# Two routed expert blocks: all six raw weight slots asked for before the passes, and the gathered rows split between the first two weight pieces

## The reference, cut to what matters

```
# moe_swiglu: each token goes to its best 2 of 8 experts
logits = xt @ w_router + b_router; top_logit, top_e = top_k(logits, 2); top_w = softmax(top_logit)
for each block of rows of one expert e:
    xb = xt[toks]
    h = silu(xb @ w_gate[e]) * (xb @ w_up[e])          # 1024 x 1408 twice
    out = (h @ w_down[e]) * w                          # 1408 x 1024
y[token] += out
# hier_moe: each token goes to its best group of 4, and to 2 experts in it
hid = silu(t @ w_gate[e]) * (t @ w_up[e]) * combine[e] # per expert 1024 x 256 twice
y = sum over e of hid @ w_down[e]                      # 256 x 1024
```

## Time and profile before

| | |
|---|---|
| median of the runs | 2325.05 us |
| profiled execution, its own time | 2320.53 us |
| its span, first to last instruction | 2319.0 us |
| PE / PEld busy | 2068.7 us (89%) / 1570.0 us (68%) |
| DVE / ACT / POOL busy | 1285.5 us (55%) / 994.2 us (43%) / 185.8 us (8%) |
| `moe` norm, plan, passes begin | 1059.7, 1085.3, 1105.1 us |
| `hm` norm, plan, passes begin | 2062.8, 2093.4, 2110.0 us |
| DMA rate, last three of the 40 slices of 58 us | 399, 373, 258 GB/s |

### The profile page before, as it was taken

How to read it: one execution, slowest core, us unless ns; L and a number is a source line. 1 busy time by engine, 2 the same in 40 slices (tenths; PEclk the granted TensorE clock), 3 DMA queues, 4 the chain that set the end, 5 groups by cost and what they waited for, 6 DMA issues and landing times. The chain is left out here.

```text
span 2319.0 us, 31287 instructions
## 1 busy us (share of the span) xinstructions
PE 2068.7 (89%) x11611; PEld 1570.0 (68%) x11611; DVE 1285.5 (55%) x1814; ACT 994.2 (43%) x1308; POOL 185.8 (8%) x182
## 2 busy tenths in 40 slices
PE   7966898889999989997899999997898789686998
PEld 5743334668888877876777888786476359575776
DVE  3367746353133234444566666888367745525888
ACT  2135736342223222221566665774243643404774
POOL 0010000000000000000311010111112200002111
PEclk9978988989999999997899999999999789886999
DMA  8006101144144125002778777995320000126996
GB/s 249 6 14 237 47 10 45 37 127 123 43 122 127 37 83 194 1 37 83 256 269 282 278 270 281 370 391 216 88 73 28 12 1 1 74 84 174 399 373 258
DMA packets 220713, 336.29 MB, mean 145 GB/s; under 512 B 50413, under 2 KB 135309, under 8 KB 220606
## 3 DMA queue, kind: packets, MB, share of 16 engines
q1 hardware_dynamic: 213470, 314.53, 40.0%
q0 software_dynamic: 7136, 20.34, 2.3%
HBM read 306.82 MB, written 26.95 MB: 144 GB/s over the span
## 5 line engine op out<-in xcount | busy, mean ns | idle before, releaser
L1526 DVE TENSOR_TENSOR moe_pass_wL<-moe_pass_w,moe_pass_wH 128x2048 fp32r<-128x2048 f32 (+1 forms) x144 | 303.4, 2112 | 115.8 <-ACT moe_pass_wH L1450 111.3
L1450 ACT ACTIVATE moe_pass_wH<-moe_pass_w 128x2048 fp32r<-128x2048 f32 (+1 forms) x144 | 254.7, 1772 | 129.6 <-PE PS L557 97.2
L555 PE MATMUL PS<-moe_pass_wL,moe_pass_xgH 128*128 128x512 f32 (+1 forms) x384 | 148.3, 386 | 9.1 <-DVE moe_pass_xgL L1531 4.8
L1526 DVE TENSOR_TENSOR hm_pass_wL<-hm_pass_w,hm_pass_wH 128x2048 fp32r<-128x2048 f32 x60 | 135.9, 2288 | 34.8 <-ACT hm_pass_wH L1450 34.7
L555 PE MATMUL PS<-xnT_low,ffn_upH 128*128 128x512 f32 x352 | 140.3, 399 | 7.4 <-DVE xnT_low L873 7.1
L557 PE MATMUL PS<-moe_pass_wH,moe_pass_xgH 128*128 128x512 f32 (+1 forms) x384 | 143.5, 374 | 0.0
L556 PE MATMUL PS<-moe_pass_wH,moe_pass_xgL 128*128 128x512 f32 (+1 forms) x384 | 143.5, 374 | 0.0
L557 PE MATMUL PS<-ffn_xH,ffn_upH 128*128 128x512 f32 x352 | 139.9, 397 | 0.0
L556 PE MATMUL PS<-ffn_xH,ffn_up_low 128*128 128x512 f32 x352 | 138.4, 393 | 0.0
L1450 ACT ACTIVATE hm_pass_wH<-hm_pass_w 128x2048 fp32r<-128x2048 f32 x60 | 112.2, 1910 | 17.1 <-PEq L1340 6.0
L880 DVE TENSOR_TENSOR ffn_hT<-ffn_sg,PS 128x512 f32<-128x512 f32 x22 | 15.1, 688 | 167.7 <-PE PS L557 167.7
(11 more groups left out here) (841 smaller groups left out, 4868.6 us busy)
## 6 DMA issues: line engine op xcount, KB each, us to landing
moe_pass_w<-in_moe_w_down SPq DMA_DIRECT2D x40, 1024.0 KB, 4.9
moe_pass_w<-in_moe_w_gate SPq DMA_DIRECT2D x32, 1024.0 KB, 5.2
moe_pass_w<-in_moe_w_up SPq DMA_DIRECT2D x32, 1024.0 KB, 7.2
hm_pass_w<-in_exp_w_gate SPq DMA_DIRECT2D x40, 512.0 KB, 7.7
hm_pass_w<-in_exp_w_up SPq DMA_DIRECT2D x40, 512.0 KB, 6.9
hm_pass_w<-in_exp_w_down SPq DMA_DIRECT2D x40, 512.0 KB
od_W<-in_od_w_in SPq DMA_DIRECT2D x12, 1024.0 KB, 8.2
moe_pass_w<-in_moe_w_gate SPq DMA_DIRECT2D x16, 768.0 KB
```

What stands on the lines that cost most here:

```text
L555: nc.tensor.matmul(out, lh, rl, start=start, stop=False)
L1450: nc.scalar.activation(wH[:, i % S, 0:n], w[:, i % R, 0:n], ACT.Copy).then_inc(s["high"], 1)
L1526: nc.vector.tensor_tensor(wL[:, i % S, 0:n], w[:, i % R, 0:n], f32(wH[:, i % S, 0:n]), ALU.subtract) \
```

## The change: what it does

`first` asks for all `R` = 6 items instead of two, in `moe` in the plan stage and in `hm` in the norm stage, so in `hm` 12 DMAs of 512 KB instead of 4 stand ahead of the four stores of `xs`. The four loads at the passes' start are gone. On ACT the rows' rounding `xg_high` goes between `high(0, 0)` and `high(0, 1)` in `hm` alone; in `moe` (where `OVER` is 32) ACT's order stays. On DVE `xg_low` goes between `low(0, 0)` and `low(0, 1)` in both. The passes after the first and the loop's body are as they were.

```diff
@@ class ExpertWeights @@
     def first(self, sp, e):
-        for i in range(self.AHEAD):
+        for i in range(self.R):
             self.load(sp, e, i)
@@ sorted_passes, block.sync @@
             n = passes(sp)
-            e = expert(sp, 0)
-            for i in range(AHEAD, R):
-                ring.load(sp, e, i)
@@ sorted_passes, block.scalar @@
             high(0, 0)
-            high(0, 1)
+            if OVER:
+                high(0, 1)
             xg_high(0, OVER > 0)
+            if not OVER:
+                high(0, 1)
@@ sorted_passes, block.vector @@
             low(0, 0)
+            xg_low(0)
             low(0, 1)
             if NW:
                 dve.sem_inc(s["cw"], 1)
-            xg_low(0)
```

## The result

The changed kernel took **2309.05 us** (2304.84 to 2317.68, six runs) beside 2322.74 for the kernel before (2315.34 to 2329.28, six runs): ratio 0.9947, 95% interval 0.9922 to 0.9973. Forecast were 2317.8 us and a range of 2312.5 to 2323.5: right in sign, too small, and outside the range. The profiled execution took 2309.62 us (span 2307.9) against 2320.53 (2319.0): 10.9 us less. Over all 13 executions of the changed kernel in this study the mean is 2311.3 us, over 100 of the kernel before 2323.7: **-12.4 us**.

What follows compares the result with a forecast made beforehand. PE sets the pace inside the passes, so only its idle or slow time at the two starts can be won. -2.2 - 5.4 + 0 + 0, less 0.3 allowance, gives -7.3: 2325.05 to 2317.8 us, range 2312.5 to 2323.5.

Steps and rivals of the forecast that it cites:

- the allowance: Taken off the summed gain for cover thinner than it looks, item 2's low part being ready only 2 us early: 0.3 us.
- Term 1: Start of `hm`'s passes: rows rounded before item 1, so PE's first product starts sooner: -2.2 us.
- the clock's rise: `hm`'s first pass: how soon PE's clock rises after the first product, put at nothing with +-1 us kept for it.
- rival C: `hm`'s first pass stays bound by DMA, items 6 and on come late: only -4.0 us, 2321.0; chance 0.12.
- Term 2: `hm`'s first pass: four loads moved ahead remove the 3.86 us stall and its slow clock: -5.4 us, bounds 3.9 to 5.6.
- Term 3: `hm`'s norm stage: twelve load DMAs ahead of the row stores, which land later but with 8.8 us of cover: cost 0.
- Rival D: `hm`'s row stores land too late for the gather if loads run below 160 GB/s: 9 us slower, 2334; chance 0.07.
- Terms 4 and 5: `moe`'s start: earlier rows on DVE win 1.7 us, six loads delaying the gather 2.0 us give it back: together 0.
- B: `moe`'s gather is hit hard by the loads, rows 4.6 us late, +2.6 us there: 2320.4; chance 0.12.

Runs made afterwards that it cites:

- own-wait kernels: Changed kernel with the gain's load on its own semaphore, so rows need not wait for router loads: in `hm` 2309.57 us; in both blocks 2302.64, again 2309.77.
- own-wait run on before: Kernel before, with DVE in `hm`'s norm stage waiting for the gain's load alone before making the rows: 2313.01 us, ratio 0.9956.
- the run with the router load put back: Changed kernel with two small loads more on SP's queue ahead of the router's in `hm`'s norm stage: 2315.76 us, ratio 0.9962.
- six-ahead-in-`moe` kernel: Kernel before with the new order in both blocks and six items' loads ahead in `moe` alone, two in `hm`: 2322.91 us, ratio 0.9999.

## Why the prediction was wrong, point by point

**The base, and the stretch from ACT's first rounding in `hm` to pass 2.** 47.69 us in the forecast's own profile, 50.5, 50.4 and 48.9 in three more; 41.0, 43.4 and 42.6 in the changed kernel. On the means 49.4 to 42.3: -7.1, where terms 1 and 2 gave -7.3 with the allowance. The sum was right by luck: its split was wrong, and two errors cancelled:
- *Term 1, the order in `hm`, -2.2.* The chain came out exactly (5.6 instead of 7.8 us) but brought nothing net: 49.1 us with the order alone against 49.4, and a mean of 42.3 with both against 42.3 for the loads alone (one profile each of the partial kernels). The step that failed is that the pass was taken to keep its length when it starts sooner. The forecast had put the clock's rise at nothing; it came 6.0, 3.0 and 4.8 us behind the first product, where the four profiles of before had 3.4, 3.2, 2.9 and 3.3. That is 1.4 us later on the mean, and at half speed 0.7 us lost. And PE came to item 7 before it had landed: 2.37 and 1.49 us of waiting in two of three profiles. This is the mechanism of rival C, at a smaller price.
- *Term 2, the loads, -5.4.* Measured -7.1 (49.4 to 42.3, loads alone). The stall of 3.86 us came from the luckiest of four profiles (the others had 5.1 to 5.8 us of such waits), and 5.6 was not the most that could be won: the later passes' 36.8 us are no floor, since a first pass of 34.3 to 34.5 occurs.
- *Term 3, queue and stores.* No cost, as forecast, but with less cover than 8.8 us. The twelve loads took 8.8 us to issue (3.09 + 3.58 + 2.15) and not 5.6, so the last store was issued at 2081.13 and landed at 2095.96, against a gather at 2097.16: about 1 us of cover, 7 and 4.5 in the other two profiles. Rival D's mechanism was real, its price and threshold wrong: it did not need 160 GB/s, only a norm stage of 18.7 or 17.0 us instead of 29.3, as the own-wait kernels had. It then costs 1.4 and 3.5 us, not 9.
- *Terms 4 and 5, `moe`, 0.* Order alone -1.8 us at the first product (forecast -1.7), the gather delayed by 3.0 (forecast 2.0), together +1.0 at the first product and +0.5 on the stretch to pass 2. Within the bounds of -1.7 to +2.6. The turns between queues that the Trainium skill (*DMA: Bandwidth & Descriptors*, Queues, rings and completion order) describes gave 1.6 us of delay when worked out in the forecast; the trace shows 3.0, so that estimate of equal shares was too low.

**The step that put the time outside the range** is one that is not there: `hm`'s norm stage was priced by its queue alone (term 3, cost 0), as "late by 1.8 us at most" for the stores; nothing was put down for when its first row comes or for its clock. It shrank from 29.3 us to 22.2, 28.0 and 26.0, on the mean by 3.9. Of this 0.9 us is the first row, which waits for the last router load, and 3.0 us the time from there to the scores, in which PE's clock was partly full in two of the three profiles and never in before. The own-wait run on before shows that the stage is on the path and worth 4 us and more; the run with the router load put back has the late row, but its time does not settle the first share. Why SP is through sooner is only argued. The change takes four loads from the start of `moe`'s passes and so shifts SP's code. In every kernel without them SP's second load begins 0.35 us into the stage, in every kernel with them at 0.68. The last router load's issue, beside which a packet of the instruction queue (q8) falls 3 to 4 us into the stage, took 0.90 to 1.31 us in five of the profiles without them, but 2.1 to 2.4 us in the six others, the changed kernel's third profile among these, and 1.8 to 2.4 in all with them. Where the router load was quick, the four weight loads behind it took 2.9 to 3.1 us instead of 1.8 to 2.1: the delay falls on the next loads, for which the first row does not wait. That the change brings the full clock is not shown either: the same program had both in two executions. With the wait as it was and no transposes added, the time from first row to scores was under 21.7 us in four of six profiles with twelve loads ahead in `hm` and in one of seven with four, too few to tell a cause.

**The remainder.** From its start to the end `hm` took 256.2, 259.9, 259.1 and 259.1 us in the profiles of before and 242.2, 251.2 and 248.6 in those of the changed kernel: -11.2 on the means, which is the 7.1 of the passes' start, the 3.9 of the norm stage and 0.2 of the plan stage. So nearly all of the -12.4 lies in this block. From 2317.8 to 2309.6 (the median of 13) are 8.2 us: 1.4 from the median of three that stood 1.4 above the mean of 100, 1.7 because the median of the 13 lies below their mean, 3.9 from the norm stage. Of the last 1.2 us, 0.2 is the plan stage, the passes and `moe` gave 0.7 less than forecast, and 1.7 I can't place, within what untouched stages move between executions (from `moe`'s last product to `hm`'s start 449.0 to 452.1 us in four profiles of before). Of the rivals B did not occur: the gather cost 3.0 us, not 4.6. C occurred in part: ACT waited for item 7 in all three profiles, and PE in two.

## What to carry to other kernels

Before you move requests to an earlier stage, read that stage as well: what its first work waits for, and which semaphore bundles loads that are not needed at the same time. Here one wait that took the router's loads with the gain's was worth as much, each alone on the kernel before (-10.0 us on the mean), as all the weight loads moved ahead (-10.3), and cost no transfer. A product that starts sooner is no gain until the pass behind it is seen to end sooner: the clock was still low, and a later piece had not landed. And take a stall from several profiles, before and after: the single one here was the smallest of four, and the single one of the changed kernel had none where two others had.

## What the runs showed of the hardware that was not expected

- **Small scatters slow large loads.** POOL's four scatters of slots (128 numbers each, to DRAM) were issued from 2110.7 to 2118.5 in before, and the weight loads ran at 170 GB/s in 2115 to 2120 and 118 in 2125 to 2130 with the DMA engines busy (share 0.93 to 1.11). With the scatters gone from there the loads ran at 409 GB/s right behind the first product, in one profile. The Trainium skill (*DMA: Bandwidth & Descriptors*, Specifications) gives 512 bytes as the least transfer for full rate and says that below it the engine reads, modifies and writes. No run here shows that step itself. What the trace shows is that the others pay: from 2110 to 2130 the loads' packets of 4 KB took 321 ns on the mean (median 159, longest 3.7 us), and 163 ns from 2135 to 2140.
- **A gather of 0.65 MB beside loads lands 3.0 us later**: 6.83, 6.75 and 6.80 us after POOL's second issue with six loads of 1 MB in flight, 3.84 and 3.73 with two.
- **SP's issue of a 512 KB load is no constant**: four took 1.86 us in the earlier trace rows, and 3.09, 3.58 and 2.15 us in the changed kernel. How many are asked for does not decide it alone: with only four asked for the six-ahead-in-`moe` kernel took 3.02 us, and the first four of twelve took 1.86 us with two ahead in `moe`.
- **More PE work ahead of a stage does not bring its clock by itself**: with 18 transposes more the stretch from first row to scores took 21.0 and 21.2 us, where it is 21.7 at 1.2 GHz throughout and 12.85 at 2.4.
